# Two more column groups of gate and up as seven block products, and a closing in another order

## What is computed

```
D_FF = 2816

def swiglu(x, w_gate, w_up, w_down):
    return (jax.nn.silu(x @ w_gate) * (x @ w_up)) @ w_down

def half_ffn(h, l, j):
    y = swiglu(rms_norm(h, ffn_norm_pre[l, j]), ffn_w_gate[l, j], ffn_w_up[l, j], ffn_w_down[l, j])
    return h + 0.5 * rms_norm(y, ffn_norm_post[l, j])

for l in range(DEPTH):
    h = half_ffn(h, l, 0)
    ...
    h = half_ffn(h, l, 1)
```

## Time and profile before

| | us |
|---|---|
| median of 3 runs | 2297.38 |
| lowest and highest | 2297.29, 2299.59 |
| the profiled execution's own time | 2296.25 |
| its span, first to last instruction | 2294.2 |

### The profile page before, as it was taken

How to read it: one execution, slowest core, us unless ns; L and a number is a source line. 1 busy time by engine, 2 the same in 40 slices (tenths; PEclk the granted TensorE clock), 3 DMA queues, 4 the chain that set the end, 5 groups by cost and what they waited for, 6 DMA issues and landing times. The chain is left out here.

```text
span 2294.2 us, 32607 instructions
## 1 busy us (share of the span) xinstructions
PE 2263.9 (99%) x12963; PEld 1969.6 (86%) x12963; DVE 1483.9 (65%) x1913; ACT 1049.5 (46%) x1627; POOL 103.3 (5%) x145
## 2 busy tenths in 40 slices
PE   8999999999999999999999999999999999999998
PEld 7888888888888888889988889988878888888997
DVE  5757445586545658577757567746896575756774
ACT  5433324444544444436544435535265554343552
POOL 0000003100000000000010000000000000000000
PEclk9999999999999999999999999999999999999999
DMA  4342332321223233415534315543322213431562
GB/s 169 104 135 74 99 106 73 113 68 59 74 74 101 65 127 131 142 51 140 167 126 166 124 42 147 166 156 92 101 75 83 92 65 98 150 124 59 132 173 110
DMA packets 181757, 249.84 MB, mean 109 GB/s; under 512 B 13832, under 2 KB 125800, under 8 KB 181608
## 3 DMA queue, kind: packets, MB, share of 16 engines
q1 hardware_dynamic: 177176, 232.00, 31.2%
q0 software_dynamic: 4320, 15.73, 3.5%
q10 hardware_dynamic: 112, 0.03, 0.0%
HBM read 222.54 MB, written 9.44 MB: 101 GB/s over the span
## 5 line engine op out<-in xcount | busy, mean ns | idle before, releaser
L2476 PE MATMUL ps<-xlo,whi 128*128 128x512 f32 (+1 forms) x1936 | 671.0, 347 | 7.7 <-issue 5.7
L2478 PE MATMUL ps<-xhi,whi 128*128 128x512 f32 (+1 forms) x1936 | 668.1, 345 | 0.0
L2477 PE MATMUL ps<-xhi,wlo 128*128 128x512 f32 (+1 forms) x1696 | 600.3, 354 | 0.0
L1532 DVE TENSOR_TENSOR wlo<-raw,whi 128x1024 fp32r<-128x1024 f32 x251 | 306.3, 1224 | 321.4 <-ACT whi L916 318.6
L916 ACT ACTIVATE whi<-raw 128x1024 fp32r<-128x1024 f32 x281 | 294.9, 1054 | 342.9 <-PE ps L2478 301.1
L2476 PEld LDWEIGHTS ps<-xlo,whi 128*128 128x128 f32 x1936 | 367.5, 190 | 53.2 <-issue 9.2
L2478 PEld LDWEIGHTS ps<-xhi,whi 128*128 128x128 f32 x1936 | 367.3, 190 | 44.1
L2477 PEld LDWEIGHTS ps<-xhi,wlo 128*128 128x128 f32 x1696 | 321.4, 190 | 43.6
L1538 DVE SCALAR_TENSOR_TENSOR wlo<-raw,vec,whi 128x512 fp32r<-128x512 f32 (+1 forms) x224 | 154.7, 735 | 154.2 <-ACT whi L920 153.6
L920 ACT ACTIVATE whi<-raw,vec 128x512 fp32r<-128x512 f32 (+1 forms) x224 | 145.4, 702 | 197.9 <-PE ps L2478 163.2
L2476 PE MATMUL ps<-wlo,xhi 128*128 128x512 f32 x352 | 138.7, 394 | 1.0 <-issue 1.0
(11 more groups left out here) (323 smaller groups left out, 3829.7 us busy)
## 6 DMA issues: line engine op xcount, KB each, us to landing
raw<-ffn_w_gate_dram SPq DMA_DIRECT2D x176, 256.0 KB, 3.1
raw<-ffn_w_up_dram SPq DMA_DIRECT2D x176, 256.0 KB, 3.2
raw<-ffn_w_down_dram SPq DMA_DIRECT2D x96, 256.0 KB, 2.9
w<-ffn_w_down_dram SPq DMA_DIRECT2D x72, 256.0 KB, 5.3
raw<-xattn_w_kv_dram SPq DMA_DIRECT2D x64, 256.0 KB, 3.0
lo_aside<-raw POOLq DMA_DIRECT2D x30, 512.0 KB, 5.1
raw<-even_w_in_dram SPq DMA_DIRECT2D x56, 256.0 KB, 2.9
raw<-odd_w_in_dram SPq DMA_DIRECT2D x42, 256.0 KB, 2.9
```

The lines of the kernel that those rows point to most:

```text
L1532: v.tensor_tensor(flat(wlo[:, slot]), flat(raw[:, from_slot]), flat(whi[:, slot]).bitcast(f32), SUB).then_inc(lo_made, 1)
L2476: mm(out_ap, lh, rl, start=start, stop=False, skip_group_check=skip_group_check)
L2477: mm(out_ap, ll, rh, start=False, stop=False, skip_group_check=skip_group_check)
L2478: return mm(out_ap, lh, rh, start=False, stop=stop, skip_group_check=skip_group_check)
```

## The change

The list of groups gets 3 and 4, for the last three feed-forwards. The second stage is then two woven groups and a plain group 5. `c12` gets a place of its own, in the fourth quarter of `ring`, whose first three quarters hold `w12` there; ACT's wait for `mid_lo_ready` moves from the copy of c12 to the write into `mid` at the group's end. In `close_sublayer` of ACT, where a feed-forward follows, the square of tile 1 moves ahead of the scaling of tile 0's rows.

```diff
-WOVEN = (6, 7, 8, 9, 10)
+WOVEN = (3, 4, 6, 7, 8, 9, 10)
...
+    c12 = place("c12", [P, 2, HALF], f32, ring_at + 3 * SEQ * FLOAT)
...
                 next_h(0)
+                square_tile(kind, second, 1, done + n)
                 scale_rows(0)
-                square_tile(kind, second, 1, done + n)
                 split_next()
...
-            act.wait_ge(mid_lo_ready, 2 * (mids - 1))
-            keep(2, c12, x_out)
+            keep(2, c12[:], x_out)
...
             act.wait_ge(pieces_used, base + len(WOVEN_UNITS) + SPLIT_SLOTS)
+            act.wait_ge(mid_lo_ready, 2 * (mids - 1))
             a(c21, x_out, ACT.Silu).then_inc(gate_silu, 1)
...
-            E.run(v.tensor_tensor(c12, z_out, c12, ADD))
+            E.run(v.tensor_tensor(c12[:], z_out, c12[:], ADD))
...
-            v.tensor_tensor(u12, c11[:], c12, MUL)
+            v.tensor_tensor(u12, c11[:], c12[:], MUL)
```

More of the change, by code:

```diff
@@ L1219, in weave @@
             x_out, z_out = [PS[:, b, :].rearrange("p (f n) -> p f n", f=2) for b in (bank, bank + 2)]
-            c12, c21 = halves_of(mid[:, 0:4, :], 0), halves_of(mid[:, 4:8, :], 1)
+            c21 = halves_of(mid[:, 4:8, :], 1)
             def keep(unit, dst, src):
@@ L2025, in weave @@
             x_out, y_out, z_out = [PS[:, bank + b, :].rearrange("p (f n) -> p f n", f=2) for b in range(3)]
-            c12, u12 = halves_of(mid[:, 0:4, :], 0), halves_of(mid[:, 4:8, :], 0)
+            u12 = halves_of(mid[:, 4:8, :], 0)
             c21 = halves_of(mid[:, 4:8, :], 1)
```

## The result

The changed kernel takes 2308.66 us (median of four runs, 2306.41 to 2310.84) beside 2297.34 for the kernel before: a ratio of 1.0045, with a 95% interval of 1.0032 to 1.0058. It is slower by 11.3 us where 2.8 us faster was forecast, and lies 5.7 us above the stated range.

A forecast was written before the change was run, and what follows sets the result against it. PE, busy 99% of the span, was taken as the bound; -9.6 (columns) + 3 x (2.2 start + 0.4 DVE) - 1.0 (closing) = -2.8 us took 2297.38 to 2294.6 us, range 2288.5 to 2303.0.

The forecast's parts named there:

- The columns: Groups 3 and 4 of three feed-forwards on PE: 21.76 to 20.16 us each, 9.6 us less in all.
- ACT: ACT in the middle stage's groups: two extra high parts and the moved wait for the low half cost nothing.
- The start of group 4: PE waits for B11's accumulate at group 4's start: 2.2 us per feed-forward, bounds 1.3 to 6.2.
- B': Start of group 4: accumulate not held at all, lands after 4.4 us, nothing waits; -10.6, 2286.8 us; chance 0.10.
- rival C: Group 4: down weights' corners go ahead of the accumulate, stall 6.2, late B21 1.2; +11.6, 2309 us; chance 0.15.
- the late slot of the last paragraph: Group 4: B11's corner's slot may free later than between groups 6 and 7; each us past 13.70 adds to the stall.
- DVE and T4: DVE's extra 2.6 us of block work delays the c22 sum ahead of T4: 0.4 us per feed-forward, bounds 0 to 1.2.
- The closing: End of layer 0, transposes after tile 1's earlier square: 1.0 us less; cross-attentions 0; bounds -1.4 to +0.8.

The follow-up runs named there:

- the kernel with the late copy and the corners in group 5: Changed kernel, B21's negated copy made on ACT just ahead of B21's own high part, down weights' corners loaded in plain group 5: 2284.82 us, 0.9939.

## Why the prediction was wrong

**The columns: right.** Seven products in place of eight give 20.15 to 20.23 us for a group wherever nothing waits, and in the kernel with the late copy and the corners in group 5 the six groups take 122.8 us where six plain ones take 130.6. That is 7.8 of the 9.6 us, with 1.67 of the rest in one wait.

**ACT: this step failed.** I priced ACT by its busy time, 12.3 of 20.2 us, and by the one wait that the change moves, and wrote "nothing". What counted was its order: B21's negated copy stands early in it and waits for a load, and everything behind it waits along. The trace of before had the sign, 29.6 us of ACT waiting at that copy, and I didn't read that row. The term is 3.2 to 3.5 us at T2 in each feed-forward, some 10 us, and it isn't in the sum. (The moved wait cost nothing, as forecast, but not for the reason given: the 1.4 us of the earlier trace rows are at the copy of c12, its old place.)

**The start of group 4: right in kind, too large.** 2.2 was forecast; 0.97, 1.16 and 0.78 us came, below my lower bound of 1.3. The accumulates took 8.1, 8.6 and 8.4 us, near the row I chose, but POOL issued them 13.12 us after the group's start and not 13.70: in the earlier trace rows ACT's copy ahead of the issue had stood 0.6 us for a load. And where T4 of group 3 had already waited, less was left at the start. I wrote that sharing the engines would make the wait shorter than I took. But twice the shortest 4.4, my own estimate for sharing, is the 8.7 that I took, and B' with its 4.4 is no sharing at all. I looked for the price of the corners on POOL's queue. Most of it fell on SP's own queue instead, on the load behind them. A late B21 stood only in rival C, and the late slot of the last paragraph was that of the wrong corner.

**DVE and T4: right in size, for another reason.** 0.4 us a feed-forward was forecast for DVE's block work. PE waited ahead of T4, by starts, 0, 0.87 and 0.58 us in the changed kernel: 0.42 and 0.58 in group 3, 0.45 in group 4 of the second feed-forward. But no block sums stand ahead of group 3's T4. DVE stood there for a load of the up weights behind the corners, and with the corners moved this wait is gone; so the agreement is luck. Where only group 4 is changed the order costs 1.1 us, at T2 and not at T4.

**The clock: not in the sum.** About 1.4 and 1.5 us behind two of the three waits.

**The closing: right by the traces, not told by the times.** The wait at its place fell by 1.2 us, where 1.0 was forecast, and the time of the closing alone is the same within 2 us.

**Rival C** had the sign, the place and, with 2309, the time. Its sum had the parts reversed: it gave 6.2 us to the start and 1.2 to B21, and the runs show about 1 and 3.3, with the clock behind; so that its 2309 met the time is luck. It got 0.15, since I counted a late B21 as a small mishap at the end of the group.

The spans of the two profiled executions, 2294.2 and 2304.3, differ by 10.1 us. Groups 3 and 4 explain 8.3 of it, and the closing takes about 1 back. Some 2.8 lie in a stage that both kernels share, where the granted clock of 18 us (580 to 598) was 0.91 before and 0.72 after; kernels with and without the change show either value, so that I don't put it down to the change. The medians differ by 11.3 us, by the interval 7.4 to 13.3; how much of them is that stage's clock stays open.

## What to carry to other kernels

An engine that is busy 60% of the time is still the bound where its next instruction waits for a load: before adding loads to a queue, follow who waits for the last of them, and what stands behind that waiter in its own order. A step that is done early "to be ready" should not wait for anything that comes late. And when a change brings a transfer-hungry form of work into a stage that already has its own transfers, move these out first: the same change lost 11 us with the corners in group 4 and won 7 with them in group 5.

## What the hardware showed

The nine loads of the corners cost SP's own next load more than POOL's accumulate beside them. With the corners ahead of it, B21's loads took 7.5 to 9.2 us in the three feed-forwards, against 4.0 to 6.8 with the corners in group 5 and the copy still early, and they were issued 3.3 to 3.7 us later after group 3's start. The accumulate took 8.1 to 8.6 us against 6.9 to 7.4. The 8.1 to 8.6 us are about twice the shortest of 4.4. That would fit the turns between queue rows that the Trainium skill states ("DMA: Bandwidth & Descriptors", section "Queues, rings and completion order"), but no run here tells turns from another cause of delay. The accumulate for group 4's B11 varied much: over all kernels with both groups changed it took 7.6 to 10.3 us with the corners in group 4, 6.9 to 9.9 with them behind B21, and 6.8 to 8.6 with them in group 5.

Of three waits of PE of 3.2 to 3.5 us, two were followed by some 3 us at a granted clock of about 0.5 and one was not. The stretch table behind the third and the second, the clock in the third column from the end:

```profile
2071.76:2075.00 3.24, 3.24 (x15) 3.24 (x16) 2.99 (x4) 1.90 (x2) 0.00 (x0) 0.51 0.03 5
1329.01:1332.00 2.99, 2.99 (x25) 2.99 (x26) 2.73 (x4) 1.65 (x2) 0.00 (x0) 1.00 0.00 0
```

In nearly the same time 15 matmuls ran in the one and 25 in the other. The same kernel can win or lose 1.5 us there, and a forecast of a wait of this length should hold both.
